# Hybrid encoder step on one core: a twelfth block pair takes two gate tiles out of the attention, another opening, another order at the memory keys

## What is computed

```
z = x @ w_in                               # 1024 -> 6416 columns, split among all branches
A: linear attention (4 heads, 64-frame blocks, low-rank forget gate)
B: sliding-window attention (8 query heads, 2 key heads, window 128, sinks, partial rotary)
C: attention into 256 memory tokens (keys and values = mem @ w_mem_kv)
mix = (g_a*y_a + g_b*y_b + g_c*y_c) @ w_o  # g = sigmoid(gate columns of z), 3 x 1024
x = LN1(alpha*x + mix);  x = LN2(alpha*x + ConvFFN(x))
```

## Time and profile before

| | |
|---|---|
| median of 3 runs | 1761.74 us (1761.08 to 1762.87) |
| profiled execution | 1763.0 us, its span 1760.9 us |
| PE busy | 1726.4 us, 98% |
| DVE busy | 1088.1 us, 62% |
| ACT busy | 758.1 us, 43% |
| mean granted TensorE clock | 0.993 |

### The profile page before, as it was taken

How to read it: one execution, slowest core, us unless ns; L and a number is a source line. 1 busy time by engine, 2 the same in 40 slices (tenths; PEclk the granted TensorE clock), 3 DMA queues, 4 the chain that set the end, 5 groups by cost and what they waited for, 6 DMA issues and landing times.

```text
span 1760.9 us, 31777 instructions
## 1 busy us (share of the span) xinstructions
PE 1726.4 (98%) x12136; PEld 1669.9 (95%) x12136; DVE 1088.1 (62%) x1555; ACT 758.1 (43%) x1366; POOL 218.2 (12%) x319
## 2 busy tenths in 40 slices
PE   8999999999998999999999999999999999999997
PEld 7999999999996899899997889999999999999997
DVE  5644432666644766556665788777776776644564
ACT  6433332445432655563341245544445544443342
POOL 0000000000000200000000023333333331002011
PEclk9999999999999999999999999999999999999999
DMA  5333328422436311125553232222222223874662
GB/s 164 110 98 114 117 86 257 113 73 74 135 92 181 120 50 48 48 72 147 142 184 113 84 88 84 87 72 85 72 72 72 72 72 113 264 265 164 214 229 74
DMA packets 191506, 207.84 MB, mean 118 GB/s; under 512 B 21526, under 2 KB 152407, under 8 KB 191415
## 3 DMA queue, kind: packets, MB, share of 16 engines
q1 hardware_dynamic: 189558, 200.60, 36.7%
q0 software_dynamic: 1856, 5.99, 0.9%
HBM read 157.43 MB, written 48.53 MB: 117 GB/s over the span
## 4 chain that ended last, share of the span: by engine, by line
PE 65%; DVE 4%; issue 1%; ACT 1%; DMA 1%; SPq 0%; POOL 0%; ACTq 0%; POOLq 0%; DVEq 0%
PE banks L1676 24%; PE banks L1179 10%; PE banks L1180 10%; PE banks L1181 10%; PE banks L1633 5%; PE banks L1470 1%; PE banks L1487 1%; PE banks L1450 1%; PE banks L1482 1%; PE banks L1455 1%; DMA w_raw<-in_w_mem_kv 1%; PE banks L1644 0%; DVE wo L2802 0%; DMA h_raw<-h_keep 0%; PE banks L1610 0%
## 5 line engine op out<-in xcount | busy, mean ns | idle before, releaser
L1179 PE MATMUL banks<-act_hi,w_hi 128*128 128x352 f32 (+1 forms) x672 | 225.8, 336 | 9.1 <-ACT z L1785 4.7
L1676 PE MATMUL banks<-x_free_r,a_hi 128*128 128x256 f32 x1232 | 226.7, 282 | 0.8 <-DVE a_lo L2912 0.5
L1181 PE MATMUL banks<-act_hi,w_lo 128*128 128x352 f32 (+1 forms) x672 | 219.7, 327 | 0.0
L1180 PE MATMUL banks<-act_lo,w_hi 128*128 128x352 f32 (+1 forms) x672 | 219.5, 327 | 0.0
L1676 PEld LDWEIGHTS banks<-x_free_r,a_hi 128*128 128x128 f32 x1232 | 190.1, 188 | 1.3 <-DVE x_free_r L2938 0.7
L1676 PE MATMUL banks<-xs_hi,a_hi 128*128 128x274 f32 x616 | 178.8, 290 | 1.7 <-DVE xs_lo L2938 1.1
L1676 PE MATMUL banks<-xs_lo,a_hi 128*128 128x274 f32 x616 | 178.4, 290 | 0.0
L1676 PE MATMUL banks<-xs_hi,a_lo 128*128 128x274 f32 x616 | 178.3, 289 | 0.0
L1676 PE MATMUL banks<-x_free_r,a_lo 128*128 128x256 f32 x616 | 173.4, 281 | 0.0
L1180 PE MATMUL banks<-h_lo,w_hi 128*128 128x384 f32 (+1 forms) x448 | 147.3, 329 | 0.0
L1179 PE MATMUL banks<-h_hi,w_hi 128*128 128x384 f32 (+1 forms) x448 | 146.9, 328 | 0.2 <-DVE h_lo L3077 0.2
(11 more groups left out here) (352 smaller groups left out, 4320.8 us busy)
## 6 DMA issues: line engine op xcount, KB each, us to landing
w_raw<-in_w_down SPq DMA_DIRECT2D x112, 256.0 KB, 3.5
w_raw<-in_w_in SPq DMA_DIRECT2D x80, 256.0 KB, 3.7
gate_in<-gates_scratch SPq DMA_DIRECT2D x24, 529.0 KB, 3.8
h_keep<-conv SPq DMA_DIRECT2D x22, 530.0 KB, 2.7
gates_scratch<-zu SPq DMA_DIRECT2D x11, 1058.0 KB, 7.1
w_raw<-in_w_up SPq DMA_DIRECT2D x44, 256.0 KB, 3.9
x_free<-in_w_up SPq DMA_DIRECT2D x44, 256.0 KB, 3.6
h_raw<-h_keep SPq DMA_DIRECT2D x22, 384.0 KB, 5.3
```

The lines of the kernel that those rows point to most:

```text
L1179: pe.matmul(out, hi, b_hi, start=start, stop=False)
L1180: pe.matmul(out, hi, b_lo, start=False, stop=False)
L1181: return pe.matmul(out, lo, b_hi, start=False, stop=stop)
L1676: last = pe.matmul(out, a[j][:, k, :], x[s][j][:, k, :], start=fresh and k == 0 and n_ == 0, stop=k == 3 and n_ == 2, skip_group_check=True)
```

## The change

- **Opening.** PE multiplies a tile of zeros 17 times before x arrives (a new memset of `z_sum` on DVE, first in its queue, and one more count on `cleared`), and does 24 transposes of `ident` behind the third `x_turn`, in place of nine before the first.
- **Twelfth pair.** NZ is 12; pair 11 makes gate tiles 22 and 23. It uses the other set of buffers and banks, so what follows it changes its bank (`Z_LAST`).
- **Attention.** 18 slices of six gate tiles are left; the steps in `ATT_BARE` have none. Splits follow the slices, so some stand in other steps than before. The loops over i are written out.
- **Memory keys.** T_MQ_B goes between the second and the third key tile on PE, ACT, DVE and SP; SP brings back z row 9 and the window keys ahead of key tiles 2 and 3; ACT copies the T_MQ_B slices ahead of the split of T_MV.

```diff
-NZ = 11
+NZ = 12
+Z_LAST = (NZ - 1) % 2
-Z_GATES = (12, 14, 6, 8)
+Z_GATES = (12, 14, 6, 8, 22)
+ATT_BARE = ((0, 5), (1, 2), (1, 5), (2, 2), (2, 5), (3, 2))
+ATT_FILL = [(i, j) for i in range(5) for j in range(6) if (0, 3) <= (i, j) <= (4, 2) and (i, j) not in ATT_BARE]
...
-T_MK = T_MQ + 1
-T_MQ_B = T_MQ + 5
+T_MK = (T_MQ + 1, T_MQ + 2, T_MQ + 4, T_MQ + 5)
+T_MQ_B = T_MQ + 3
...
@@ sync: memory keys
-        mem_tile(2)
+        cols(T_MQ_B // 2, T_MQ_B % 2, w_in, C_MQ + 3 * P)
...
-        mem_tile(3)
-        cols(T_MQ_B // 2, T_MQ_B % 2, w_in, C_MQ + 3 * P)
         sp.dma_start(z[:, 9, :], gates[A_KEEP + 9]).then_inc(q.z_back, 16)
         sp.dma_start(kpad[:, P:P + TT], gates[A_KEEP + 8]).then_inc(q.z_back, 16)
+        mem_tile(2)
+        mem_tile(3)
...
-        last = gate_loop(T_GATE_B // 2, 16, 4, gate_st2, PS_GATE_B)
+        last = gate_loop(T_GATE_B // 2, 16, 3, gate_st2, PS_GATE_B)
@@ tensor: opening
+        pe.wait_ge(q.cleared, 1)
+        for _ in range(17):
+            pe.matmul(bank(0)[:, 0:P], z_sum[0][:, 0, :], z_sum[0][:, 1, :], start=True, stop=True)
         pe.wait_ge(q.consts, 16)
-        for _ in range(9):
-            pe.transpose(bank(0)[:, 0:P], ident[:, :], ident[:, :])
         for t in range(3):
             x_turn(t)
+        for _ in range(24):
+            pe.transpose(bank(0)[:, 0:P], ident[:, :], ident[:, :])
@@ tensor: pairs (scalar and vector alike)
-        with pe.Fori(1, NZ // 2) as i:
+        with pe.Fori(1, (NZ - 1) // 2) as i:
             z_pair(i * 2, 0)
             z_pair(i * 2 + 1, 1)
-        z_pair(NZ - 1, 0)
+        z_pair(NZ - 2, 0)
+        z_pair(NZ - 1, Z_LAST)
@@ tensor: memory keys
-        for i in range(4):
-            mem_tile((T_MK + i) // 2, (T_MK + i) % 2, 0, i)
+        for i in range(2):
+            mem_tile(T_MK[i] // 2, T_MK[i] % 2, 0, i)
         tile_start(T_MQ_B // 2, T_MQ_B % 2)
         for gi in range(3):
             proj_slice(PS_MQ_B + gi, (PS_MQ_B + gi) % 2, T_MQ_B % 2, gi)
+        for i in range(2, 4):
+            mem_tile(T_MK[i] // 2, T_MK[i] % 2, 0, i)
@@ tensor: attention
         def gate_slice_b(i, j, beside=None):
-            if j % 3 == 0:
-                tile_start(i + (T_GATE_B // 2 + j // 3 - 1), 1 - j // 3)
-            proj_slice(i * 6 + (PS_GATE_B + j - 3), (PS_GATE_B + j - 3) % 2, 1 - j // 3, j % 3, beside)
+            s = att_fill(i, j)
+            if s is None:
+                return
+            f = s // 3
+            if s % 3 == 0:
+                tile_start((T_GATE_B + f) // 2, f % 2)
+            proj_slice(PS_GATE_B + s, (PS_GATE_B + s) % 2, f % 2, s % 3, beside)
...
-        with pe.Fori(1, NT // 2 - 1) as i:
+        for i in range(1, NT // 2 - 1):
             att_steps(i, False, False)
@@ scalar: memory keys
-        split_hi((T_MK + 1) // 2, 0)
-        split_hi((T_MK + 2) // 2, 1, used=(q.mem_used, 1))
-        split_hi((T_MK + 3) // 2, 0, used=(q.mem_used, 2))
-        split_hi(T_MQ_B // 2, 1, used=(q.mem_used, 3))
+        split_hi(T_MK[1] // 2, 0)
+        split_hi(T_MQ_B // 2, 1, used=(q.mem_used, 1))
+        proj_out(PS_MQ_B, PS_MQ_B % 2, 7, 0)
+        split_hi(T_MK[2] // 2, 0, used=(q.mem_used, 2))
+        proj_out(PS_MQ_B + 1, (PS_MQ_B + 1) % 2, 7, 1)
+        split_hi(T_MK[3] // 2, 1, used=(q.proj_done, PS_MQ_B + 3))
+        proj_out(PS_MQ_B + 2, PS_MQ_B % 2, 7, 2)
+        split_hi(T_MV // 2, 0, used=(q.mem_used, 3))
         for t in range(2):
             act.wait_ge(q.proj_done, PS_MK + t + 1)
             act.activation(mk_rows[:, t, :], bank(6 + t), ACT.Copy).then_inc(q.proj_free, 1)
-        split_hi(T_MV // 2, 0)
-        for gi in range(3):
-            proj_out(PS_MQ_B + gi, (PS_MQ_B + gi) % 2, 7, gi)
@@ scalar: attention (vector alike)
+        def next_gate(i, j):
+            s = att_fill(i, j)
+            if (i, j) == (0, 2):
+                split_hi(T_GATE_B // 2, 1)
+            elif s is not None and s % 3 == 2:
+                split_hi((T_GATE_B + s // 3 + 2) // 2, s // 3 % 2)
...
-                if j % 3 == 2:
-                    split_hi(i + (T_GATE_B // 2 + b), 1 - b)
+                next_gate(i, j)
```

More of the change, by code:

```diff
@@ L568, in raw_count @@
         if par:
-            return 384 if isinstance(c, int) and c < 2 else c * 32 + 352
+            return 448 if isinstance(c, int) and c < 2 else c * 32 + 416
         return 32 * (W0 + 1) if isinstance(c, int) and c < 2 else c * 16 + 32 * (W0 + 1)
@@ L743, in mem_tile @@
         def mem_tile(n_):
-            h, k2, tile = n_ // 4, n_ % 4, (T_MV + n_ - 4 if n_ >= 4 else T_MK + n_)
+            h, k2, tile = n_ // 4, n_ % 4, (T_MV + n_ - 4 if n_ >= 4 else T_MK[n_])
             load(tile // 2, tile % 2, [(flat(tile % 2, s, 512), w_kv[:, 2 * k2 + s, 512 * h:512 * h + 512]) for s in range(2)])
@@ L851, in _ @@
         merge_tile(T_MERGE // 2, 1, BRANCHES[1], 0)
-        last(3, (0,))
+        last(2, (0,))
         sp.wait_ge(q.staged, 2 * NT + 2)
@@ L855, in _ @@
         gate_back(0)
-        last(3, (1,))
+        last(2, (1,))
         for s in range(3):
-            sp.wait_ge(gate_stored[s], 16 * (10 + NFILL))
+            sp.wait_ge(gate_stored[s], 16 * (8 + NFILL))
         for k in range(12):
@@ L1303, in _ @@
         for gi in range(3):
-            proj_slice(PS_Z + gi, 3 + 4 * (gi % 2), 0, gi)
+            proj_slice(PS_Z + gi, bank_a(1 - Z_LAST, gi % 2), 0, gi)
         for s in range(2):
@@ L1912, in _ @@
         z_window(1, 1)
-        with act.Fori(1, NZ // 2) as i:
+        with act.Fori(1, (NZ - 1) // 2) as i:
             z_window(i * 2, 0)
             z_window(i * 2 + 1, 1)
+        z_window(NZ - 2, 0)
         for k in range(3):
             for s in range(2):
-                z_snap(NZ - 1, 0, s, k)
+                z_snap(NZ - 1, Z_LAST, s, k)
         split_hi(1, 0, used=(q.prod_mm[1], z_count(NZ - 1, 0)))
         for s in range(2):
-            z_snap(NZ - 1, 0, s, 3)
+            z_snap(NZ - 1, Z_LAST, s, 3)
         split_hi(1, 1, used=(q.prod_mm[1], z_count(NZ - 1, 4)))
@@ L1932, in _ @@
         for gi in range(3):
-            gate_out(PS_Z + gi, 3 + 4 * (gi % 2), gi, gate_st, 0)
+            gate_out(PS_Z + gi, bank_a(1 - Z_LAST, gi % 2), gi, gate_st, 0)
             if gi == 1:
@@ L2073, in gate_out_b @@
         def gate_out_b(i, j):
[L2074 removed]
+            s = att_fill(i, j)
+            if s is not None:
+                gate_out(PS_GATE_B + s, (PS_GATE_B + s) % 2, s % 3, gate_st2, 2 + NFILL + s // 3)
+        def next_gate(i, j):
+            s = att_fill(i, j)
+            if (i, j) == (0, 2):
+                split_hi(T_GATE_B // 2, 1)
+            elif s is not None and s % 3 == 2:
+                split_hi((T_GATE_B + s // 3 + 2) // 2, s // 3 % 2)
         def att_steps(i, first, last):
@@ L2103, in _ @@
         att_steps(0, True, False)
-        with act.Fori(1, NT // 2 - 1) as i:
+        for i in range(1, NT // 2 - 1):
             att_steps(i, False, False)
@@ L2442, in split_lo @@
             dve.tensor_tensor(dst[:, :, :], w_raw[slot][:, :, :], src[:, :, :].bitcast(F32), ALU.subtract).then_inc(q.w_split_lo, 1)
+        dve.memset(z_sum[0][:, 0:2, :], 0.0).then_inc(q.cleared, 1)
         dve.memset(eps[:, :], LN_EPS)
@@ L2564, in _ @@
         z_window(1, 1)
-        with dve.Fori(1, NZ // 2) as i:
+        with dve.Fori(1, (NZ - 1) // 2) as i:
             z_window(i * 2, 0)
             z_window(i * 2 + 1, 1)
+        z_window(NZ - 2, 0)
         for k in range(3):
             for s in range(2):
-                z_combine(NZ - 1, 0, s, k)
+                z_combine(NZ - 1, Z_LAST, s, k)
             if k == 0:
@@ L2774, in att_steps @@
                     split_lo(T_GATE_B // 2, 0)
-                if j % 3 == 2:
-                    split_lo(i + (T_GATE_B // 2 + j // 3), 1 - j // 3)
+                s = att_fill(i, j)
+                if (i, j) == (0, 2):
+                    split_lo(T_GATE_B // 2, 1)
+                elif s is not None and s % 3 == 2:
+                    split_lo((T_GATE_B + s // 3 + 2) // 2, s // 3 % 2)
         def branch_lo(place):
@@ L2786, in _ @@
         att_steps(0, True, False)
-        with dve.Fori(1, NT // 2 - 1) as i:
+        for i in range(1, NT // 2 - 1):
             att_steps(i, False, False)
```

26 lines of the change are left out of this document (14 added, 12 removed).

## The result

| | median | against the kernel before, same chips |
|---|---|---|
| before | 1762.07 us (4 runs) | |
| after | 1781.99 us (4 runs) | 1.0113, 95% interval 1.0096 to 1.0131 |

The account below looks back on a forecast made before the run. TensorE, busy 1726.4 of 1760.9 us, was taken as the bound, but bare attention steps as held by the softmax chain. -3.0 + 20.65 - 0.6 + 8.4 - 11.2 = +14.25 us gave 1776.0; 8 times in 10 between 1766 and 1785.

Parts of the forecast that it names:

- opening: Program start: zero matmuls and transposes raise the clock earlier and fill the split gap; -3.0 us, between -1.5 and -3.6.
- twelfth pair: Block pairs: one more pair, for gate columns 22 and 23, adds +20.65 us, given 20.5 to 21.0.
- slices left out: Six attention steps without dense work: a bare step saves only 0.1 us; in sum -0.6 us, between 0 and -2.
- clock behind six holes: Attention: TensorE idles 3.9 us per bare step, then works at a lower clock; 6 x 1.4 = +8.4 us, bounds 0 and 16.
- memory keys: Key tiles and memory query: two waits and their slow stretches go; -11.2 us, range -11.8 to -8.
- the 7.2 us chain of the softmax: Bare step: from the scores' end through mask, exponentials, scaling and copy to the value product, 7.2 us without the slice.
- the price from the earlier trace: Work behind a wait is slower: 1.3 us more for 12 key-tile matmuls, 1.5 us more for a slice.
- the bound of 2.7 from the opening: Attention holes: if the clock stays down as long as in the opening, 6 x 2.7 = 16 us, 1783.8; chance 0.10.
- covered by a load: Opening: 17 zero matmuls take 4.1 us while the x tile lands at 5.03, so they cost 0 to 0.2 us.
- the first value tile: Memory keys: named as late next, key copies queued behind its split; if it comes 2 us late, 2 us are lost.
- The rival on the other side: Attention: slices were on TensorE's path, 23.9 us go, no hole opens and the clock holds; 1744.3, chance 0.05.
- Each microsecond cut from the chain would give 6: Bare steps: each microsecond cut from the 7.2 us softmax chain would give 6 us.

Follow-up runs that it names:

- hold_22: The changed kernel with 22 matmuls of 128 x 352 in each of the six holes, ahead of the mem value product, results thrown away: 1772.5 us.
- gates_only: The kernel before with the moved gate tiles alone (twelfth block pair, six steps without dense work): 1792.5 us, ratio 1.0169 to before.
- hold_11: The changed kernel with 11 matmuls at the beginning of each of the six holes, leaving holes of 2.2 us: 1775.2 us, ratio 1.0069 to before.
- keys_only: The kernel before with the new order of the memory keys alone: 1752.5 us, ratio 0.9931 to before.
- copy_both: The changed kernel; in bare steps VectorE copies turned probabilities ahead of the next unit's scaling, ScalarE its half ahead of the next unit's exponentials: 1765.6 us.
- copy_bare: The changed kernel, in whose six bare steps VectorE alone copies the turned probabilities ahead of the scaling of the next unit: 1766.8 us.
- no_move: The kernel before with 10 opening zero matmuls, new key order and two queue edits at the keys, without moved gate tiles or reordered steps: 1747.7 us.

## Why the prediction was right, and where it was off

Forecast +14.25 us, 1776.0; measured 1782.0, inside 1766 to 1785. Slower was given 0.93. Term by term, against the stages of the two traces:

| term | forecast | measured |
|---|---|---|
| opening | -3.0 (-1.5 to -3.6) | -2.0 |
| twelfth pair | +20.65 | +20.65 |
| slices left out | -0.6 (0 to -2) | 0.0 |
| clock behind six holes | +8.4 (0 to 16) | +11.5 |
| memory keys | -11.2 (-8 to -11.8) | -9.6 |
| last linear tile, tail | 0 | -2.3 |

- **What bounds the bare step** was read rightly: the 7.2 us chain of the softmax, not the slice. The waits are where and as long as forecast (six of 3.9 us, ended by VectorE's copy of the probabilities), and hold_22 shows by experiment that TensorE work of that length is free there. The value product stands where it stood, to 0.01 us, so the slices are worth 0.0 us, where the forecast had -0.6.
- **The clock** is the term that was mis-sized: +8.4 us in the forecast, +11.5 measured. Four holes cost 1.4 to 1.6 us over before, as the price from the earlier trace rows says; two cost 2.65 and 2.71, what the bound of 2.7 from the opening had. The forecast took one price for all six; the spread among equal holes, which gates_only and hold_11 show again, was in its two ends only. The Trainium skill's page TensorE: Matmul & The Clock Gate, section "HAM oscillation — how this bites in real kernels", says that a wait that recurs in a loop is paid for with a cold stretch each time; the six windows of after agree (0.77 to 0.88 in each). The waits in that section are some 3 to 5 us long, so it says nothing of the shorter holes of hold_11, of which three of six were followed by the lower clock.
- **The opening** came out at -2.0 us in place of -3.0, and one step of it failed: 17 zeros at 0.24 us each, 4.1 us, "covered by a load". Each leaves two records and the 17 take 6.4 us, so the turn of x is 2.4 us late and the first slice 0.85 us. The forecast let them cost 0 to 0.2, and its sign for this, a first slice 2 to 3 us earlier, did not come. With ten zeros the three kernels start the block pairs at 43.2 to 43.5 us, 3.0 us ahead of the mean of the three with the old opening (46.3); the eight with 17 are 1.7 us ahead (mean 44.6). So the whole term was there to be had, with fewer zeros.
- **The keys**: both waits and both slow stretches went, 11.6 us from the memory rows to the first scores. The forecast named what is late next, the first value tile with the key copies queued behind its split, and counted nothing for it; it took back 2.0 us, with a wait of 1.8 us where the forecast's sign was none over 1. keys_only shows the same wait, 1.7 us. How much the late tile costs is chance in part: among the eight kernels with this order the stretch from the turn of the memory rows to the first turned unit takes 43.5 to 46.4 us, with after at 44.2 and before at 53.8.
- **The last linear tile** was held to be no part of the change, and it is none: it takes 1.6 us more or less in kernels whose instructions up to there are the same (from the last matmul of the pairs to the turn of the memory rows 248.6 us in after and hold_22, 250.1 in copy_both). A single trace carries this much chance, here in favour of after. Of -0.7 us behind the attention the cause was not looked for.
- **The rival on the other side** (slices on the path, 1744.3) needed a chain shorter than 3.4 us. The forecast put it on one place in VectorE's order. That was too simple: ScalarE's copy behind the exponentials is as much a member (copy_bare), and with both moved the wait came back a step later (copy_both). "Each microsecond cut from the chain would give 6" held for the first 1.6 us (copy_bare, 9.8 us less of waits) and beyond that only where the next unit's mask and maximum are moved too: 8.43 us for the bare step and 7.7 behind it.
- **A source read too simply.** The formula that the prediction quotes from the Trainium skill (TensorE: Matmul & The Clock Gate, "Back-to-back issue gap") stands there for isolated matmuls, and the section gives other figures for streams with a weight load each. The sum went by the trace's 123 ns, so nothing in it changes.
- **How much was luck.** The median lies 6.0 us above the forecast. By the spans it is 4.0 us (18.2 for 14.25); the other 2 are the spread of executions, since the profiled one of before lay 1.3 us above its median and that of after 0.8 below. Of the sizes, the clock (+3.1), the keys (+1.6), the opening (+1.0) and the slices (+0.6) all missed to the slow side, and the last linear tile and the tail (-2.3), which the forecast left at nothing, took some of it back.

## What to carry to other kernels

Before dense work is taken out of a step because it is wanted elsewhere, look at what ends last in that step without it: here a chain on two other engines was as long as the slice, so 24 us of saved matmuls gave nothing, and the holes cost another 11.5 us in clock. If the work has to move, first put the releasing copies at the head of every queue they stand in, and then look one step further, since what they passed is late there. Otherwise leave the filling where it hides the chain: no_move got the whole gain of 15 us from the opening and the order at the keys.

## What the runs showed of the hardware

- Equal holes do not cost the same. Six holes of 3.9 us were all followed by lower clock, four at a loss of 1.4 to 1.6 us and two of 2.7; of six holes of 2.2 us (hold_11) three cost 1.5 to 1.6 us and three nothing; of six of 2.3 us (copy_bare) four cost 1.5 to 1.7 us and two nothing. In gates_only six holes of 3.9 us cost 1.3 to 2.8 us, the dearest in other places than in after. At the keys a wait of 1.8 us in after was followed by clock 1.00, one of 2.7 us in hold_22 by 0.68. Thirty transposes of 128 columns in the hole kept the clock at 1.00 as well as 22 matmuls of 352.
- A matmul of fp32 zeros, 128 x 128, leaves two records where a transpose by the identity leaves one: 34 for 17, 20 for 10. At the start of the program the 17 took 5.7 (hold_22) to 7.0 us (copy_both).
- The view of waits can name the wrong releaser when the right one is the instruction before it on the same engine: `vt` at 624.5 in copy_bare, where the product needs the copy at 623.98.
